# Attention's output product in three passes of split operands, w_out split in the first units, branch rows and preparation's loads moved

## What is computed

```python
p = h @ w_in                                      # rows x 3072: a 256, b 256, q 512, k 512, v 512, gate 1024
q, k = rope(rms_norm(q)), rope(rms_norm(k))       # 4 heads, 2 maps of 64
s = einsum('bhmqd,bhmkd->bhmqk', q, k) * 64 ** -0.5
P = softmax(s); P = P[:, :, 0] - lam * P[:, :, 1]
o = rms_norm(P @ v, subln_g) * (1 - lam_init)     # keys: 256 of the context and 1024 latent
y = concatenate([fourier_mix(a), pool_mix(b), o]) # 256 + 256 + 512
x = x + gate * ((y * silu(g)) @ w_out)            # 1024 x 1024
```

## Time and profile before

| | |
|---|---|
| median of three runs | 5051.18 us (5050.5 to 5054.47) |
| the profiled execution | 5054.27 us |
| its span, first to last instruction | 5052.5 us |
| mean granted TensorE clock | 0.963 |
| TensorE busy (matmul, weight load) | 4564.5 us (90%), 3603.7 (71%) |
| VectorE, ScalarE, GpSimd busy | 2260.9 (45%), 1715.3 (34%), 631.5 (12%) |
| output product, L1196 | 576 records, 262.2 us busy |
| split projection, L316, two largest forms | 1024 + 896 records, 399.9 + 353.6 us busy |
| DMA | 476.59 MB, 94 GB/s on average |

### The profile page before, as it was taken

How to read it: one execution, slowest core, us unless ns; L and a number is a source line. 1 busy time by engine, 2 the same in 40 slices (tenths; PEclk the granted TensorE clock), 3 DMA queues, 4 the chain that set the end, 5 groups by cost and what they waited for, 6 DMA issues and landing times. The chain is left out here.

```text
span 5052.5 us, 59016 instructions
## 1 busy us (share of the span) xinstructions
PE 4564.5 (90%) x23377; PEld 3603.7 (71%) x23377; DVE 2260.9 (45%) x2799; ACT 1715.3 (34%) x3151; POOL 631.5 (12%) x598
## 2 busy tenths in 40 slices
PE   8998799799889799999999986887588887999999
PEld 2886566488656488888888866886477774788887
DVE  1314677431577531111110117879577766433433
ACT  1212555331355321111112116664445422333222
POOL 0101200110300010000011003456011111000000
PEclk9999899999999999999999998999799998999999
DMA  7226201222411232222222211111201108333322
GB/s 267 98 95 216 101 26 38 104 97 96 164 71 38 75 105 88 98 100 100 100 96 96 97 72 40 51 55 55 93 18 34 34 9 316 121 103 114 117 92 84
DMA packets 245595, 476.59 MB, mean 94 GB/s; under 512 B 32264, under 2 KB 72296, under 8 KB 244988
## 3 DMA queue, kind: packets, MB, share of 16 engines
q1 hardware_dynamic: 245376, 473.61, 27.2%
HBM read 357.14 MB, written 116.41 MB: 94 GB/s over the span
## 5 line engine op out<-in xcount | busy, mean ns | idle before, releaser
L484 DVE TENSOR_TENSOR p_wl<-p_raw,p_wh 128x2048 fp32r<-128x2048 f32 x96 | 219.8, 2292 | 1013.1 <-ACT p_wh L408 1013.1
L408 ACT CAST p_wh<-p_raw 128x2048 fp32r<-128x2048 f32 x96 | 183.0, 1909 | 830.0 <-PE p_ps L316 802.8
L316 PE MATMUL p_ps<-p_wh,him 128*128 128x512 f32 x1024 | 399.9, 391 | 2.8 <-DVE p_wl L484 2.8
L316 PE MATMUL p_ps<-p_wl,him 128*128 128x512 f32 x1024 | 399.2, 390 | 0.0
L316 PE MATMUL p_ps<-p_wh,lom 128*128 128x512 f32 x1024 | 399.2, 390 | 0.0
L316 PE MATMUL p_ps<-p_wh,hi 128*128 128x512 f32 x896 | 353.6, 395 | 23.6 <-DVE p_wl L484 23.6
L316 PE MATMUL p_ps<-p_wl,hi 128*128 128x512 f32 x896 | 351.3, 392 | 0.0
L316 PE MATMUL p_ps<-p_wh,lo 128*128 128x512 f32 x896 | 351.1, 392 | 0.0
L412 ACT ACTIVATE p_stg<-p_ps 128x512 f32<-128x512 f32 x216 | 129.0, 598 | 633.6 <-PE p_ps L316 606.4
L316 PE MATMUL p_ps<-lom,p_wh 128*128 128x512 f32 x768 | 298.8, 389 | 0.0
L316 PE MATMUL p_ps<-him,p_wl 128*128 128x512 f32 x768 | 298.8, 389 | 0.0
(11 more groups left out here) (370 smaller groups left out, 9764.2 us busy)
## 6 DMA issues: line engine op xcount, KB each, us to landing
p_raw<-w_in SPq DMA_DIRECT2D x96, 1024.0 KB, 5.8
pn_dram<-p_stg SPq DMA_DIRECT2D x128, 256.0 KB, 2.0
spare<-w_down SPq DMA_DIRECT2D x32, 1024.0 KB, 4.8
spare<-w_up SPq DMA_DIRECT2D x30, 1024.0 KB, 5.3
p_dram<-p_stg SPq DMA_DIRECT2D x112, 256.0 KB, 2.2
m_w<-w_mod SPq DMA_DIRECT2D x12, 2048.0 KB, 11.8
pt_dram<-p_stg SPq DMA_DIRECT2D x96, 256.0 KB, 2.0
z_ogm<-pn_dram SPq DMA_DIRECT2D x48, 512.0 KB, 13.8
```

Source lines behind the costliest of these rows:

```text
L316: mm = pe.matmul(ps[:, u, :], lhsT, rhs, start=(kk == 0 and q == 0), stop=(kk == KD - 1 and q == 2))
L408: act.copy(wh[:, kh], raw[:, kh]).then_inc(s_wh[kh], 1)
L484: dve.tensor_tensor(wl[:, kh], raw[:, kh], wh[:, kh], ALU.subtract).then_inc(s_wl[kh], 1)
```

## The change

In attention w_out is no longer one float32 tile. SP loads it in eight pieces of 128 rows through the two buffers of g; ScalarE rounds each to `wh`, VectorE subtracts to `wl`, two pieces in each of the units 0 to 3. The copy of turned y now rounds to `yTh`, and VectorE makes the rest `yTl` from the same PSUM bank, ahead of the maxima of unit h = 2. Each product matmul becomes three: yTh·wh + yTh·wl + yTl·wh. The transposes that reuse the banks now wait for the subtraction. g and x of tiles 0 and 1 are loaded when w_out is through. `mixf` is private to `prepare`, is stored to DRAM there and loaded by tile beside g. `df` is gone (the difference overwrites the first map's probabilities), one modulation gate row is held instead of two, and the context's is loaded behind the store of tile 7. The head sums end with one more drain.

In the projection `first_loads` becomes three parts: columns and tables behind the first chunk, q and k rows behind the fourth chunk, and the context's branch rows (layer 0 only) where all stood before.

```diff
-                early = min(1, whole) if next_loads and q == len(plan) - 1 else whole
-                for front, a, z in ((True, 0, early), (False, early, whole)):
+                cut = min(1, whole) if next_loads and q in (0, len(plan) - 1) else whole
+                for part, a, z in ((0, 0, cut), (1, cut, whole)):
                     if z > a:
                         with sp.Fori(a, z) as i:
                             for b in range(group):
                                 step(s, i, b, s, group * i + b + 2)
-                    if front and next_loads and q == len(plan) - 1:
+                    if next_loads and (q == 0 or part == 0):
                         for x in range(SG):
-                            sp.wait_ge(s_st[x], 16 * ((s["n0"] + early * group * s["per"]) // SG + 1))
-                        sp.wait_ge(s_lA, NN)
-                        sp.wait_ge(s_lD, NN)
-                        next_loads(sp)
+                            sp.wait_ge(s_st[x], 16 * ((s["n0"] + z * group * s["per"]) // SG + 1))
+                        if q == 0 and part == 0:
+                            sp.wait_ge(s_lA, NN)
+                            sp.wait_ge(s_lD, NN)
+                        next_loads[2 if q > 0 else part](sp)
...
-    def first_loads(sp):
-        sp.dma_start(raw[:, 0], C.p_dram[0:P, Q0:Q0 + 1024]).then_inc(F.s_raw[0], 16)
+    def rows_ab(sp, t0, t1):
+        sp.dma_start(ab[:, t0:t1], C.p_dram[t0 * P:t1 * P, 0:2 * FW].rearrange("(t p) n -> p t n", p=P)).then_inc(F.s_ab, 16)
+
+    def first_columns(sp):
         load_dft(sp, 0)
-        sp.dma_start(ab[:], C.p_dram[0:tiles * P, 0:2 * FW].rearrange("(t p) n -> p t n", p=P)).then_inc(F.s_ab, 16)
+        rows_ab(sp, 0, NT)
         sp.dma_start(nyq[:, 0:1], ins["t_nyq"]).then_inc(F.s_ab, 16)
         sp.dma_start(gq[:].rearrange("p a b -> p (a b)"),
                      ins["qk_norm_g"][l].rearrange("a b -> (a b)").partition_broadcast(P)).then_inc(F.s_rope, 16)
         for q in range(2):
             for w in range(2):
                 sp.dma_start((cg, sg)[q][:, w], ins["t_rope"][q].rearrange("(t p) n -> p t n", p=P)).then_inc(F.s_rope, 16)
-        for n in range(1, NR):
+        sp.dma_start(chan[:], ins["t_chan"].rearrange("g p n -> p g n")).then_inc(F.s_tab, 16)
+
+    def queries_keys(sp):
+        for n in range(NR):
             sp.dma_start(raw[:, n], C.p_dram[n * P:(n + 1) * P, Q0:Q0 + 1024]).then_inc(F.s_raw[n], 16)
-        sp.dma_start(chan[:], ins["t_chan"].rearrange("g p n -> p g n")).then_inc(F.s_tab, 16)
-    F.first_loads = first_loads
+
+    def context_rows(sp):
+        if tiles > NT:
+            rows_ab(sp, NT, tiles)
+    F.next_loads = (first_columns, queries_keys, context_rows)
...
+            for t in outs:
+                sp.wait_ge(s_oc, at[t] + 1)
+                sp.dma_start(C.mix_dram[t * P:(t + 1) * P, :], mixf[:, t, :]).then_inc(s_st, 16)
+            sp.wait_ge(s_st, 16 * tiles)
...
+        wh = sb("wh", [P, KD, D], F32R)
+        wl = sb("wl", [P, KD, D], F32R)
+        yTh = sb("yTh", [P, 2, KD, P], F32R)
+        yTl = sb("yTl", [P, 2, KD, P], F32R)
         pr = sb("pr", [P, 2, 2, SEQ + CTX])
-        df = sb("df", [P, SEQ + CTX])
...
+                else:
+                    sp.wait_ge(s_wl, KD - 1 + t)
+                sp.dma_start(mix[:, t % 2, :], C.mix_dram[t * P:(t + 1) * P, :]).then_inc(s_mix[t % 2], 16)
...
+            for k in range(KD):
+                if k >= 2:
+                    sp.wait_ge(s_wl, k - 1)
+                sp.dma_start(g[:, k % 2, :], ins["w_out"][l][k * P:(k + 1) * P, :]).then_inc(s_w[k % 2], 16)
             for t in range(2):
                 load(t)
                 load_x(t)
-            sp.dma_start(w[:], ins["w_out"][l].rearrange("(k p) n -> p k n", p=P)).then_inc(s_w, 16)
-            for r in range(2):
-                sp.dma_start(gate[:, r, :], C.gate_dram[l][r].partition_broadcast(P)).then_inc(s_gate, 16)
+            sp.dma_start(gate[:], C.gate_dram[l][0].partition_broadcast(P)).then_inc(s_gate, 16)
...
+                if t == NT - 1 and tiles > NT:
+                    sp.dma_start(gate[:], C.gate_dram[l][1].partition_broadcast(P)).then_inc(s_gate, 16)
...
+                    if turned:
+                        pe.wait_ge(s_yl, 2 * (t - 1) + 1)
+                    elif n > 0:
+                        pe.wait_ge(s_tc, ring_T[n])
+                if q == 1 and turned:
+                    pe.wait_ge(s_yl, 2 * (t - 1) + 2)
...
-                    mm = pe.transpose(tp(q % 2)[:, k * P:(k + 1) * P], df[:, (first + k) * P:(first + k + 1) * P], C.ident[:])
+                    mm = pe.transpose(tp(q % 2)[:, k * P:(k + 1) * P], pr[:, n % 2, 0, (k0 + first + k) * P:(k0 + first + k + 1) * P], C.ident[:])
...
-                        pe.wait_ge(s_tc, ring_y[t] + 2)
+                        pe.wait_ge(s_yl, 2 * t + 2)
                         if t == 0:
-                            pe.wait_ge(s_w, 16)
+                            pe.wait_ge(s_wl, KD)
+                cols = slice(half * CH, (half + 1) * CH)
                 for k in range(4 * part, 4 * part + 4):
-                    mm = pe.matmul(po, yT[:, t % 2, k, :], w[:, k, half * CH:(half + 1) * CH],
-                                   start=(k == 0), stop=(k == KD - 1))
+                    for q, (y_, w_) in enumerate(((yTh, wh), (yTh, wl), (yTl, wh))):
+                        mm = pe.matmul(po, y_[:, t % 2, k, :], w_[:, k, cols], start=(k == 0 and q == 0), stop=(k == KD - 1 and q == 2))
...
+            def round_w(k):
+                act.wait_ge(s_w[k % 2], 16 * (k // 2 + 1))
+                act.copy(wh[:, k, :], g[:, k % 2, :]).then_inc(s_wh, 1)
...
+                if n < KD // 2:
+                    for k in (2 * n, 2 * n + 1):
+                        round_w(k)
...
+                dve.drain()
...
+                dve.wait_ge(s_mix[b], 16 * (t // 2 + 1))
+                dve.tensor_tensor(y[:, 0:2 * FW], mix[:, b, :], g[:, b, 0:2 * FW], ALU.mult)
...
+            def split_w(k):
+                dve.wait_ge(s_wh, k + 1)
+                dve.tensor_tensor(wl[:, k, :], g[:, k % 2, :], wh[:, k, :], ALU.subtract).then_inc(s_wl, 1)
+
+            def split_y(t):
+                for r in range(2):
+                    dve.wait_ge(s_tc, ring_y[t] + r + 1)
+                    two = (slice(None), t % 2, slice(4 * r, 4 * r + 4))
+                    dve.tensor_tensor(yTl[two], tp(r).rearrange("p (a b) -> p a b", b=P), yTh[two], ALU.subtract).then_inc(s_yl, 1)
...
+                if h == 2 and 1 <= t <= tiles:
+                    split_y(t - 1)
...
+                if n < KD // 2:
+                    for k in (2 * n, 2 * n + 1):
+                        split_w(k)
```

More of the change, by code:

```diff
@@ L608, in prepare_space @@
            ("ytc", [P, 2, 2, CTX]), ("sq", [P, 2, 2 * 512]), ("ss", [P, 2, 16]), ("rs", [P, 2, 16]), ("nrm", [P, 2, 2 * 512]),
-           ("t1", [P, 2 * 512]), ("dft1", [P, NT, CH])]
+           ("t1", [P, 2 * 512]), ("mixf", [P, tiles, 2 * FW]), ("dft1", [P, NT, CH])]
     early = [("ab", [P, tiles, 2 * FW]), ("dft0", [P, NT, CH]), ("raw", [P, NR, 2 * 512]), ("nyq", [P, 8]), ("chan", [P, 2, P]),
              ("gq", [P, 2, QK]), ("cg", [P, 2, NT, QK]), ("sg", [P, 2, NT, QK])]
-    kept = 4 * (NTA * 2 * FW + 2 * HEADS * (SEQ + CTX))
+    kept = 4 * (2 * HEADS * (SEQ + CTX))
     busy = 4 * (2 * KD * (SEQ + CTX) + 3 * KD * CH + 4 * CH)
@@ L809, in branch_out @@
                 mm.then_inc(s_o, 1)
-            pe.wait_ge(s_ab, 32)
+            pe.wait_ge(s_ab, 32 if last else 48)
             token_dft(0)
@@ L1038, in attention_out @@
         oa = sb("oa", [P, 2, HEADS * DV])
-        w = sb("w", [P, KD, D])
         g = sb("g", [P, 2, D])
-        sq = sb("sq", [P, HEADS * DV])
+        mix = sb("mix", [P, 2, 2 * FW])
         ms = sb("ms", [P, 2, HEADS])
@@ L1054, in attention_out @@
         po = ps[:, 7, :]
-        s_w = sem("w_loaded")
+        s_w = [sem(f"w_loaded{b}") for b in range(2)]
+        s_wh = sem("w_hi_ready")
+        s_wl = sem("w_lo_ready")
+        s_mix = [sem(f"branches_loaded{b}") for b in range(2)]
         s_sub = sem("subln_loaded")
@@ L1165, in turn_probs @@
                     pe.wait_ge(s_d, n + 1)
-                    if n > 0:
-                        pe.wait_ge(s_tc, ring_T[n] - 1 if turned else ring_T[n])
-                if q == 1 and n > 0:
-                    pe.wait_ge(s_tc if turned else s_oc, ring_T[n] if turned else n)
+                    if turned:
[4 more added lines that the diff above has]
+                    pe.wait_ge(s_yl, 2 * (t - 1) + 2)
+                elif q == 1 and n > 0:
+                    pe.wait_ge(s_oc, n)
                 if q == 2:
@@ L1181, in values @@
                     pe.wait_ge(s_oc, n)
+                if h == 2 and t >= 1:
+                    pe.wait_ge(s_yl, 2 * t)
                 for k in range(nk):
@@ L1338, in update @@
                 dve.wait_ge(s_po, 2 * t + half + 1)
-                if t == 0 and half == 0:
```

(8 more changed lines are left out.)

19 lines of the change are left out of this document (11 added, 8 removed).

## The result

| | before | changed |
|---|---|---|
| median | 5052.83 us (4 runs, 5050.5 to 5055.77) | 4999.39 us (4 runs, 4997.73 to 5001.21) |
| span of the profiled execution | 5052.5 us | 4998.3 us |
| mean granted TensorE clock | 0.963 | 0.963 |

What follows compares the result with a forecast made beforehand. TensorE was taken to bound projection and attention. Terms -38.2 + 8 - 20.7 - 9.1 = -60.0 us gave 4991 us against the 5051.18 median; the forecast's own range was 4977 to 5004, the wider range 4975 to 5014.

Steps and rivals of the forecast that it cites:

- signs of being wrong: Prediction wrong if h=2 units pass 12 us, units 1 to 3 pass 11, or a w_in wait remains.
- Part 3: Projection, preparation's loads in three parts: 20.7 us less in layer 0, 9.1 us less ahead of layer 1's preparation.
- C: Layer 0's projection: context segment stays short of w_in, half the stall remains, 5001 us; chance 0.08 together with F.
- F: Layer 0's projection: moved loads still meet the last segment, at C's price; chance 0.08 together with C.
- Part 1: Attention, product in three fp32r passes, with splitting of turned y in h=2 units: 38.2 us less in sum.
- Rival D: Attention's products: passes bring nothing, fp32r beside f32 starts every 0.287 us, 5029 us; chance 0.05.
- E: Attention's products: granted clock falls, passes run at 0.42 us intervals, kernel slower, 5144 us on the median; chance 0.03.
- rival A: Attention's h=2 units: splits and waits count whole, 1.4 instead of 0.65 in 16 units, 12 us, 5003; chance 0.12.
- Part 2: Attention's units 0 to 3, splitting w_out: 4 us more per layer, 8 in all; bounds 0 and 18.2 per layer.
- Rival B: Attention's units 1 to 3: halves of g are the bottleneck, 26 us more over both layers, 5017; chance 0.08.
- the slower rival: The same as E: TensorE's clock falls at attention's products, 5144 us on the median; chance 0.03.
- Part 4: Preparation's mixf stores, mix loads beside g, late context gate load, probabilities in place of df: all at no cost.

Runs made afterwards that it cites:

- the loads alone: The kernel before with only the three-part first_loads and their places in the projection, attention untouched and mixf kept in SBUF: 5023.61 us, ratio 0.9944.
- Four buffers: The changed kernel with w_out's pieces loaded through four buffers (two of g, two of x) instead of two: 4986.80 us, ratio 0.9871.

## Why the prediction was right, and where it was off

**Sign and size.** 4999.4 lies 8.4 above the 4991 and inside the range. The bound was read rightly: TensorE in both stages. Some of the closeness is luck. The stretches that the sum speaks of give 48.7 of the forecast 60; another 5.5 came from stretches where nothing was forecast. And two of the prediction's own signs of being wrong were met: the first h=2 unit of each layer took 12.17 and 12.09, over the 12 named there, and of units 1 to 3 unit 1 of layer 0 (11.25) and units 1 and 3 of layer 1 (11.94, 12.07) passed 11. Both lie in the two terms below that failed.

**Part 3, right.** -20.97 for -20.7 and -9.12 for -9.1; the loads alone gave 28.6 of 29.8. The upper end of the range for w_in (only 10 us of the stall goes) and rivals C and F fall: no idle TensorE is left in the segment. Nor did the loads behind the first chunk cost anything.

**Part 1, right in mechanism, small errors in size.** Full units h=3 and h=0 at 9.43, h=1 at 9.51, h=2 at 11.16, where 9.4, 9.6 and 11.0 stood. A piece takes 2.85, not 2.72: the starts in it lie 0.231 apart, and the first interval is 0.31. That is 0.13 a piece, and in h=3 and h=0 units little of it shows. Rival D (0.287) falls; so does E, as far as the full units go. Four passes for true float32 (the Trainium skill, FP8 and Floating Point Precision, TensorE Precision Notes) would make three passes 3/4 of the piece, the prediction's estimate; the rows give 2.85 of 3.44, which is 0.83.

One step of this part failed, the price of splitting y in the unit h=2 without a product: "a loss of 0.65 per layer". It took transposes as the path. Without a product VectorE carries this unit, and both subtractions with their waits count whole, 1.4, which is rival A's price at the one place of each layer where nothing else was long enough to cover it. With the clock it was 1.45 in layer 0 and 3.00 in layer 1: the kernel before was at the lower clock in this unit of layer 0 (10.72) and at the full one in layer 1 (9.09), the changed kernel at the lower one in both. So 2.8 of the 4.45 are the split, the rest is clock. In full units A is wrong.

**Part 2, the term that was mis-sized.** "18.8 for two units, 9.4 a unit", for three units, 4 us a layer; measured, 5.94 in layer 0 and 8.02 in layer 1 over units 1 to 4. The chain (split, load, cast, copies, exps) is what the rows show. It was counted wrongly: there are two pairs of units in it, 2 x 2.5 = 5, not 1.5 pairs. And it left out the idle TensorE in its middle, behind which the clock falls: the values of units 1 and 3 take 3.98 and 3.62 us in layer 0 and 4.63 and 4.63 in layer 1, against 2.50 at the full clock. The rest, 0.9 and 3.0, goes with that; no run separates it. The bounds given, 0 and 18.2 a layer, hold. Rival B, a bottleneck at the two buffers, is the same wait with a larger price (26 us); it was real and half of that. Four buffers show it: 12.6 us less with all the work kept. The prediction's estimate of 3.2 us for a piece of w_out was low too: behind unit 0 they landed after 3.4 to 4.7.

The clock was put down as the place of the slower rival, in full units, where it stayed at 1.00. It fell at other places, behind short idle times in unit 1, 3 and 6, and in unit 31 of layer 0, which took 10.75 and not 9.43:

```profile
863.40 2.02 PE L1205 MATMUL a_ps<-ident,a_pr 128*128 128x128 f32 x10 [1.29 <-DVE a_pr L1348]
865.08 0.78 PE L1232 MATMUL a_ps<-a_wh,a_yTh 128*128 128x512 f32 x1
865.65 0.63 PE L1232 MATMUL a_ps<-a_wl,a_yTh 128*128 128x512 f32 x1
866.08 0.63 PE L1232 MATMUL a_ps<-a_wh,a_yTl 128*128 128x512 f32 x1
```

The first interval to the next start is 0.57, the ones behind it 0.43. That the engine scales its power with use and wants matmuls back to back (the Trainium skill, Perfetto Trace Analysis, Matmul Optimizations) agrees with these rows. Why it fell just there isn't settled: the same unit of the kernel before had the same 1.29 us of idle time and kept its clock, and unit 6 of layer 0 had 2.35 us of idle time ahead of it with four buffers and in the changed kernel, and only the latter slowed. The kernel before had 2.36 there in both layers and slowed in layer 0 alone.

**Part 4, right.** Nothing was forecast for it, and nothing was lost. Preparation takes 79.69 and 69.67 us to the first scores, 80.58 and 70.46 before. The gate of the context rows is issued at 915.50, and tile 8's first update starts at 922.95, 7.5 us later and not 10.7, but the load had landed at 920.76, and the update is released by the product:

```profile
915.50 0.43 SPq L1151 DMA_DIRECT2D a_gate<-gate_dram  x1
...
920.66 0.69 DVE L1358 TENSOR_TENSOR a_up<-a_oa 128x512 f32<-128x512 f32 x1
...
922.95 0.69 DVE L1385 TENSOR_TENSOR a_up<-a_ps,a_gate 128x512 f32<-128x512 f32 x1 [0.84 <-PE a_ps L1232]
```
